# Hybrid trunk, two-map attention scores as one float32r product of stacked high and low parts that pass through DRAM

## The reference

```
s1 = einsum('bqhd,bkhd->bhqk', q[..., 0, :], k[..., 0, :]) * scale
s2 = einsum('bqhd,bkhd->bhqk', q[..., 1, :], k[..., 1, :]) * scale
p  = softmax(s1) - lam * softmax(s2)
o  = einsum('bhqk,bkhd->bqhd', p, v)
```

## Time and profile before

| | us |
|---|---|
| median of 3 runs | 2806.89 |
| lowest and highest run | 2801.25, 2812.41 |
| span of the profiled execution | 2804.2 |
| TensorE busy | 2645.0 |
| VectorE busy | 1431.9 |
| ScalarE busy | 977.4 |
| GpSimd busy | 672.0 |

### The profile page before, as it was taken

How to read it: one execution, slowest core, us unless ns; L and a number is a source line. 1 busy time by engine, 2 the same in 40 slices (tenths; PEclk the granted TensorE clock), 3 DMA queues, 4 the chain that set the end, 5 groups by cost and what they waited for, 6 DMA issues and landing times.

```text
span 2804.2 us, 56030 instructions
## 1 busy us (share of the span) xinstructions
PE 2645.0 (94%) x23988; PEld 2432.0 (87%) x23988; DVE 1431.9 (51%) x2423; ACT 977.4 (35%) x1586; POOL 672.0 (24%) x477
## 2 busy tenths in 40 slices
PE   5998999999999899999989989999999997999997
PEld 5888888888889889999978888788888997999997
DVE  5667533346523646254475674333565337254364
ACT  4251143333322444243342402333333125253352
POOL 2322131222223210211222311222232331211202
PEclk9999999999999999999999999999999998999999
DMA  8110021222233223222330100122222432223232
GB/s 340 41 46 4 3 67 54 85 85 80 74 116 127 68 80 102 86 102 98 128 135 31 39 4 19 50 87 85 70 84 85 141 99 68 83 92 105 85 104 83
DMA packets 57021, 233.87 MB, mean 83 GB/s; under 512 B 6548, under 2 KB 6708, under 8 KB 55760
## 3 DMA queue, kind: packets, MB, share of 16 engines
q1 hardware_dynamic: 53808, 206.67, 21.5%
q0 software_dynamic: 2976, 23.69, 2.3%
HBM read 221.52 MB, written 8.81 MB: 82 GB/s over the span
## 4 chain that ended last, share of the span: by engine, by line
PE 82%; DVE 9%; ACT 4%; issue 2%; DMA 1%; POOL 1%; SPq 0%; ACTq 0%; DVEq 0%; POOLq 0%
PE ps_dense L978 28%; PE ps_dense L986 15%; PE ps_dense L1831 6%; PE ps_aux L978 4%; PE ps_aux L1650 4%; PE ps_dense L1603 3%; PE ps_dense L1835 3%; PE ps_aux L1367 2%; PE ps_dense L1676 1%; PE ps_dense L1012 1%; PE ps_aux L1603 1%; PE ps_aux L1353 1%; PE ps_aux L1319 1%; PE ps_dense L1664 1%; DMA arena<-in_w_early 1%
## 5 line engine op out<-in xcount | busy, mean ns | idle before, releaser
L777 POOL TENSOR_TENSOR w_low<-w_ring,w_high 128x1024 fp32r<-128x1024 f32 (+1 forms) x206 | 493.3, 2398 | 1407.4 <-ACT w_high L1985 1400.9
L1985 ACT ACTIVATE w_high<-w_ring 128x1024 fp32r<-128x1024 f32 x200 | 211.2, 1060 | 479.6 <-PE ps_dense L978 276.0
L986 PE MATMUL ps_dense<-h_high,w_high 128*128 128x320 f32 x1024 | 243.1, 319 | 12.5 <-DVE rs L2969 5.8
L978 PE MATMUL ps_dense<-z_high,w_high 128*128 128x320 f32 x1024 | 236.9, 313 | 9.8 <-ACT w_high L1985 9.8
L978 PE MATMUL ps_dense<-h_high,w_high 128*128 128x320 f32 x864 | 207.9, 323 | 33.4 <-ACT h_high L2025 30.6
L986 PE MATMUL ps_dense<-h_high,w_low 128*128 128x320 f32 x1024 | 234.1, 310 | 0.0
L986 PE MATMUL ps_dense<-h_low,w_high 128*128 128x320 f32 x1024 | 233.6, 309 | 0.0
L978 PE MATMUL ps_dense<-z_low,w_high 128*128 128x320 f32 x1024 | 233.3, 309 | 0.0
L3110 DVE SCALAR_TENSOR_TENSOR x_res<-ps_dense,mod,x_res 128x320 f32<-128x320 f32 (+2 forms) x192 | 72.6, 433 | 310.0 <-PE ps_dense L978 310.0
L978 PEld LDWEIGHTS ps_dense<-h_high,w_high 128*128 128x128 f32 x864 | 149.3, 196 | 45.4 <-issue 36.4
L978 PE MATMUL ps_dense<-h_low,w_high 128*128 128x320 f32 x864 | 187.6, 310 | 0.0
(11 more groups left out here) (529 smaller groups left out, 5471.6 us busy)
## 6 DMA issues: line engine op xcount, KB each, us to landing
w_ring<-in_w_mlp SPq DMA_DIRECT2D x128, 512.0 KB, 3.5
w_ring<-in_w_gate SPq DMA_DIRECT2D x64, 640.0 KB, 3.9
w_ring<-in_w_late SPq DMA_DIRECT2D x64, 512.0 KB, 4.6
w_ring<-in_w_in SPq DMA_DIRECT2D x48, 512.0 KB, 3.4
w_ring<-in_w_early SPq DMA_DIRECT2D x32, 512.0 KB, 3.5
w_ring<-in_w_out SPq DMA_DIRECT2D x16, 512.0 KB, 3.5
arena<-in_dft POOLq DMA_DIRECT2D x2, 2944.0 KB, 14.1
x_kept<-x_res POOLq DMA_DIRECT2D x2, 2560.0 KB, 11.4
```

Source lines behind the costliest of these rows:

```text
L777: last = g.tensor_tensor(w_low[:, n % 2, k:k + step], ring[:, slot, k:k + step, :], w_high[:, n % 2, k:k + step].bitcast(F32), ALU.subtract)
L978: last = mm(out[:, s, 0:HALF], w_[:, par_, k, :], x_[:, k, s * HALF:(s + 1) * HALF], start=first, stop=final)
L986: last = mm(out[:, s, 0:HALF], w_[:, par_, k, :], x_[:, k, s * HALF:(s + 1) * HALF], start=k == 0 and x_ is x_high and w_ is w_high, stop= ...
L1985: a(w_high[:, n % 2], ring[:, j, 0:KC, :], ACT.Copy).then_inc(w_high_in.sem, 1)
```

## The change

The rounded part and the rest of the queries and keys are made once per layer (`q_high`, `k_high` by ScalarE, the rests in place in `d_q`, `d_k` by VectorE), stored to two DRAM tensors, and loaded back so that the 128 partitions hold four blocks of 32 rows: queries as high, high, low, low, and keys as high, low, high, low. One float32r product over the 128 rows is then the sum of all four products of parts. GpSimd's pads are gone. SyncE issues the stores and loads between the gates' loads, whose loop is written out for it. The scratch tiles of the two-map part move to where the loaded keys don't lie, and four semaphores of the delta rule become one with four steps.

```diff
-        q_pad_odd = sb("q_pad_odd", [P, 4, P])
+        q_stack_odd = sbr("q_stack_odd", [P, 4, P])
+        k_parts = nc.dram_tensor("k_parts", [P, 2 * H, KEYS], F32, kind="Internal").ap()
+        q_parts = nc.dram_tensor("q_parts", [P, 2 * H, T], F32, kind="Internal").ap()
...
+        q_high, k_high = cv(2, T), cv(2, KEYS)
...
+        def gate_behind(w):
+            return next(q for q in range(PLACES[3 * w], 5 * N_FLOW) if q % 5 == 4) // 5 + 2
...
+            def parts_store(l):
+                sp.wait_ge(*parts_ready.nth(l, 4))
+                for high, low, dram in ((q_high, d_q, q_parts), (k_high, d_k, k_parts)):
+                    for r in range(4):
+                        part = (high, low)[r // 2 if dram is q_parts else r % 2]
+                        for c in range(2):
+                            dst = dram[32 * r:32 * r + 32, 4 * c:4 * c + 4].rearrange("i g t -> g i t")
+                            sp.dma_start(dst, part[:, c]).then_inc(parts_out.sem, 16)
+            def queries_load(l, n):
+                c, tt = divmod(n, NT)
+                if n:
+                    sp.wait_ge(*queries_in.nth(l, n))
+                sp.dma_start(q_stack[n % 2].bitcast(F32), q_parts[:, 4 * c:4 * c + 4, tt * P:(tt + 1) * P])\
+                    .then_inc(queries_in.sem, 16)
...
-                with sp.Fori(0, KC) as d:
-                    for n in range(4):
-                        load(l, B_GATE + 2 * n, ins["w_gate"], bass.ds(d * 4 + n, 1), 10, d * 8)
-                        load(l, B_GATE + 2 * n + 1, ins["w_late"], bass.ds(d * 4 + n, 1), KC, d * 8)
+                for i in range(N_GATE):
+                    load(l, B_GATE + 2 * i, ins["w_gate"], slice(i, i + 1), 10)
+                    load(l, B_GATE + 2 * i + 1, ins["w_late"], slice(i, i + 1), KC)
+                    if i == 3:
+                        parts_store(l)
+                    if i == 5:
+                        sp.wait_ge(*parts_out.nth(l, 16))
+                        sp.wait_ge(*dv_ps.nth(l, 3))
+                        sp.dma_start(z_both.bitcast(F32)[:, 0:4 * T].rearrange("p (g t) -> p g t", g=4), k_parts[:, 0:4, 0:T])\
+                            .then_inc(keys_in.sem, 16)
...
+                        queries_load(l, 0)
+                        queries_load(l, 1)
+                    if i == 7:
+                        sp.wait_ge(*s_ps.nth(l, U // 2))
+                        sp.wait_ge(*keys_in.nth(l, 2))
+                        for g, at in ((4, at_mq), (6, at_mk)):
...
+                    for n in range(2, 2 * NT):
+                        if i == gate_behind(U // 2 + n - 2):
+                            sp.wait_ge(*s_ps.nth(l, U + 4 * (n - 1)))
+                            queries_load(l, n)
...
                 def score(v):
...
                     if n_maps == 2:
-                        pe.wait_ge(*q_padded.nth(l, u + 1))
+                        pe.wait_ge(*keys_in.nth(l, (2, 5 if tt == NT - 1 else 4)[c]))
+                        pe.wait_ge(*queries_in.nth(l, n + 1))
...
-                            g4 = hh * 2 + m
-                            qt, k = q_pad[u % 2][:, g4 % 4], d_k[:, g4 // 4]
+                            g = 2 * (hh % 2) + m
+                            qt, k, own = q_stack[n % 2][:, g], stacked_keys(c, g), stacked_context(c, g)
...
(ScalarE, ahead of step 0)
+                a(q_high.bitcast(F32R), d_q, ACT.Copy).then_inc(parts_ready.sem, 1)
+                a(k_high.bitcast(F32R), d_k, ACT.Copy).then_inc(parts_ready.sem, 1)
...
(VectorE, in gate 3's last part, and behind the values of step 0)
+                    if i == 3:
+                        dve.wait_ge(*parts_out.nth(l, 16))
...
+                    if w == 0:
+                        dve.wait_ge(*stored_kv.nth(l, 2))
+                        dve.wait_ge(*parts_ready.nth(l, 2))
+                        for part, high in ((d_q, q_high), (d_k, k_high)):
+                            v.tensor_tensor(part.bitcast(F32R), part, high, ALU.subtract).then_inc(parts_ready.sem, 1)
```

More of the change, by code:

```diff
@@ L211, in trunk @@
         h_low = sbr("h_low", [P, KC, T])
-        z_high = sbr("z_high", [P, KC, T])
-        z_low = sbr("z_low", [P, KC, T])
+        z_both = sbr("z_both", [P, 2 * KC * T])
+        z_high, z_low = (z_both[:, i * KC * T:(i + 1) * KC * T].rearrange("p (k t) -> p k t", k=KC) for i in range(2))
         flow = sb("flow", [P, 2 * T])
@@ L335, in trunk @@
         cv = Carve()
-        d_q, d_k, d_vf = cv(2, T), cv(2, KEYS), cv(2, T)
-        m_q, m_k = cv(H, T), cv(H, KEYS)
+        d_q, d_k = cv(2, T), cv(2, KEYS)
+        at_dvf = cv.at
+        d_vf = cv(2, T)
+        at_mq = cv.at
+        m_q = cv(H, T)
+        at_mk = cv.at
+        m_k = cv(H, KEYS)
+        at_mv = cv.at
         m_v, d_v = cv(6, 256), cv(6, 256)
@@ L411, in trunk @@
         ab_kept = signal("ab_kept", 1)
[L412 to L415, removed]
+        ab_steps = signal("delta_rule_input_steps", 4)
         g_ready = signal("g_ready", 1)
@@ L491, in trunk @@
         proj_low_in = signal("projection_low_ready", N_GATE)
-        q_padded = signal("q_zeroed_and_padded", U + 1, 1)
+        parts_ready = signal("queries_and_keys_high_and_low", 4)
+        parts_out = signal("queries_and_keys_parts_out", 16, 0, 16)
+        keys_in = signal("stacked_keys_in", 5, 0, 16)
+        queries_in = signal("stacked_queries_in", 2 * NT, 0, 16)
         lam_sum = signal("lam_sum", 1)
@@ L884, in store @@
                     pool.dma_start(dst, src).then_inc(done.sem, 16)
[L886 to L891, removed]
-                        g4 = hh * 2 + m
-                        rows = slice(32 * (g4 % 4), 32 * (g4 % 4) + 32)
-                        last = g.tensor_copy(q_pad[u % 2][rows, g4 % 4], d_q[rows, g4 // 4, tt * P:(tt + 1) * P])
-                    last.then_inc(q_padded.sem, 1)
                 pool.wait_ge(*o_ps.nth(l, 5))
@@ L901, in _ @@
                 low_part(l, 17, 17 % RING)
-                held(pool, *gdn_done.nth(l, 1))
-                for i in range(2):
-                    last = g.memset(q_pad[i], 0.0)
-                last.then_inc(q_padded.sem, 1)
                 for n in range(18, N_WIN):
@@ L920, in gate_part @@
                         low_part(l, W_GATE + i + 1, 2 * (i + 1) % RING)
[L922 to L937 removed]
+                for q in range(5 * N_FLOW):
+                    gate_part(q)
                 for i in range(N_FLOW, N_GATE):
@@ L1638, in score @@
                                 pe.wait_ge(*exps.nth(l, u))
-                            qt, k = m_q[0:96, hh, tt * P:(tt + 1) * P], m_k[0:96, hh]
+                            qt, k, own = m_q[0:96, hh, tt * P:(tt + 1) * P], m_k[0:96, hh], m_k[0:96, hh, T:KEYS]
                         else:
@@ L1651, in score @@
                         else:
-                            last = mm(out[:, 0:CTX], qt, k[:, T:KEYS], start=True, stop=True)
+                            last = mm(out[:, 0:CTX], qt, own, start=True, stop=True)
                         last.then_inc(s_ps.sem, 1)
```

63 lines of the change are left out of this document (34 added, 29 removed).

## The result

Slower: 2886.45 us median (2883.23 to 2891.31, 4 runs) against 2809.06 us (2801.25 to 2812.41, 4 runs) of the kernel before beside it, ratio 1.0277 with a 95% interval of 1.0255 to 1.03. The forecast was 2867. The profiled execution spans 2881.9 us, 77.7 more than before.

What follows compares the result with a forecast made beforehand. TensorE is busy 94%, but around the scores the chain behind them was taken to set the pace. Span 2804.2 - 22 (faster product) + 83 (store stall) = 2865, so 2867 us as median; range 2795 to 2905.

Steps and rivals of the forecast that it cites:

- Step 4: 16 stores behind gate 3's loads run on four engines, delaying gate 4's load: 41.5 us a layer lost, 83 in both.
- Step 3: Making the parts on ScalarE and VectorE falls into their idle time and costs nothing; uncovered, 6 us a layer.
- Step 1: Two-map score product in float32r: a pair takes 0.62 us instead of 2.16, bounds 0.58 to 0.90.
- Step 2: Pairs 20 to 39: the chain behind the scores lets only 11.2 us a layer through, 22 in all.
- A: Rival: stores spread over 16 engines, gate 4 costs 0 to 2 us a layer; 2786 us, chance 14%.
- B: Rival: stores run half wide, eight engines' worth, 28 to 33 us; 2812 us, chance 5%.
- C: Rival: narrow stores, but the faster product's gain of 51 us is whole; 2839 us, within the forecast's 78%.
- D: Rival: stores narrow and slow, 67 us, 11.5 us more a layer; 2890 us, within the forecast's 78%.
- E: Rival: float32r score product not faster for 128 columns, under 6 us in all; inside every case, no chance given.

Runs made afterwards that it cites:

- e3_wide_f32: e1_wide with the two-map score product read as float32 instead of float32r; 2810.06 us, ratio 1.0004 to the kernel before.
- e1_wide: Changed kernel with each of the 16 stores writing one contiguous plane, 128 partitions outermost, rearrangement left out; 2802.81 us, ratio 0.9988 to the kernel before.
- e2_eight: Changed kernel with the stores' DRAM side walking 8 blocks of 16 rows outermost, rearrangement left out; 2832.85 us, ratio 1.0098 to the kernel before.
- e6_early_half: Kernel with whole-part stores and stacking loads, plus the combine's first-map scaling moved ahead of the second exp; 2779.14 us, ratio 0.99 to the kernel before.

## Why the forecast was right, and 19 us short

- **Step 4, the stores: right, in mechanism and size.** Forecast 41.5 us a layer; measured 41.6 and 43.9, and 41.2 and 45.9 with the stores alone. Four engines (share 0.26, 104 GB/s), gate 4's load behind them, ScalarE in front of everything, and TensorE's restart at half clock all stand in the rows above. The forecast kept the load's issue at its place and put only its data behind the stores; in fact SyncE couldn't issue it either until 522.86. That changed nothing in the sum, as the data came behind the stores in both pictures. The agreement is not luck: the packets of the stores run for 57.0 us in layer 1 (480.24 to 537.25) where 55.5 were forecast, and ScalarE's copy starts 1.9 us behind them where 2.6 were allowed, of which 1 us had no row.
- **Step 3, making the parts: right.** e3_wide_f32 has all of the change but the product and the narrow shape; its pairs take what they took before, and so does the whole kernel (1.0004).
- **Step 1, the product itself: nearly.** 0.75 us a pair where 0.62 was forecast and 0.90 the upper bound. By the distance of the starts 128 columns take 0.06 us (0.08 forecast) and 512 columns 0.29 to 0.34 (0.23).
- **Step 2, what comes through: right in kind, too large. This is the term that was mis-sized.** Forecast 11.2 us a layer; measured 6.2 and 5.4. The sign to look for was an idle TensorE of about 3 us released by VectorE; it is 0.62 us behind ScalarE and 1.42 behind VectorE. Stretch by stretch in layer 1: pair 20 gave 1.0 (1.3 forecast), 27 to 29 2.0 (1.5 and a part of 0.7), 30 and 31 1.1 (1.3), 32 to 35 4.9 (3.7 and a part of 1.3). What failed stands in two places: pairs 21 to 26 gave -0.4 instead of 0.6, and 36 to 39 -2.4 instead of 0.8 and the rest. Both hold stretches in which the clock fell:

```profile
650.20:666.60 16.40, 14.37 (x121) 12.73 (x117) 11.57 (x22) 6.46 (x13) 3.12 (x2) 1.00 0.27 89
666.60:684.20 17.60, 15.57 (x120) 14.21 (x116) 11.56 (x22) 6.46 (x13) 3.12 (x2) 0.90 0.25 83
...
768.90:785.90 17.00, 15.28 (x120) 14.19 (x116) 11.17 (x23) 6.58 (x13) 3.01 (x3) 0.90 0.26 86
785.90:810.40 24.50, 20.58 (x157) 19.07 (x152) 10.85 (x28) 7.17 (x17) 4.94 (x3) 0.93 0.27 96
```

 The same stretches ran at 1.00 before. The forecast saw this price, put it in the range and took 0 for it; three stretches fell in layer 1 and four in layer 2. At 1.2 to 1.3 us each they are about 4 us of the 5.0 missing in layer 1 and 5 of the 5.8 in layer 2. The other part is pair 37, whose combine already met the low part before and which with less TensorE time in front of it waits 2.19 us instead of 1.21.
- **The sum.** Forecast for the span 2865, measured 2881.9: 10.4 us of the 16.7 are step 2, 2.5 step 4, and 3.8 the untouched code, for which the prediction had no term.
- **Rivals.** A and B were no cases of the change, but their conditions and prices held where the stores were made to move at the full rate (e1_wide) or half of it (e2_eight). C is excluded by the 6 us that the product gives. D isn't seen: the stores ran at 104 GB/s, 26 an engine if there were four. E is excluded: 128 columns take 0.06 us, where float32 took two records of 0.11 us each.

Open: how much of the clock's falls follows from the new idle time and how much would fall anyway (layer 2 of e6_early_half still has one, at 0.90, with waits of 0.9 us); and why the code behind the pairs takes longer in every trace with the float32r product.

## What to carry over

Look at the outermost walk on both sides of every added transfer: one that cuts into four runs on a quarter of the engines, and all that is queued behind it waits four times as long as its bytes suggest (57 us for 5.8 MB); move the rearrangement to the side where it keeps many rows outermost, or to transfers that nobody waits for soon. A faster product gives only what the chain behind it lets through, and the two edits are worth more together (16 to 18 us a layer) than apart (1.2 and 6.1), so judge neither alone. Where two engines start off the same event, half a microsecond in the order decides whether they meet.

## What the runs showed of the hardware that wasn't expected

- SyncE does not run ahead of narrow stores: from the fourth on it issues one per 3.03 us (320 KB) or 3.61 us (384 KB); wide ones of the same size it issued in some 0.9 us each (8 in 7.82 and 6.88 us). In both cases that is about the rate at which the bytes moved (104 and 411 GB/s).
- From GpSimd's queue the same stores ran wider than a quarter: a DMA share of 0.89 at 210 GB/s from 512.5 to 517 us with no load beside, and all 16 out within 44 us of the first issue (488.41 to 532.01) with two gates' loads among them.
- A VectorE instruction of 0.88 us took 2.87 to 3.09 us beside GpSimd's 2.4 us, in 7 of 16 cases a layer; in e6_early_half the worst was 1.32.
